# Block 1's first half in another order: eight heads beside the weight slabs, one step a slab, and 512-column matmuls

## The chip, the cores and the metric

One core of one Trainium2 chip runs the whole program in one launch. The metric is the device time of a run in microseconds (us); the kernel before took 3679.07 us, the median of three runs from 3676.93 to 3680.88.

## What is computed

Two pairs of transformer blocks over 256 tokens of width 2048, all in fp32. Activations are kept transposed, with features on the 128 partitions and the 256 tokens on the free axis. One layer of "block 1" is, in the reference (cut):

```python
for i in range(DEPTH):                       # DEPTH = 2
    z = rmsnorm(x, g_mix[i]) @ w_in[i]       # 2048 -> 4928 columns
    (zq, zkv, zkr, sc_b, sc_c, sc_h, cf_a, cf_g, rq, rk, rv, rg) = split_cols(z, IN_SIZES)
    y_a = mla_group(zq, zkv, zkr, ...)       # 4 heads: q, kv from norms of zq, zkv; softmax
    y_b = sc_b * causal_dwconv(sc_c * sc_h, w_sc[i])
    u = causal_dwconv(cf_a * jax.nn.sigmoid(cf_g), w_cf[i], b_cf[i])   # 31 taps
    y_c = jax.nn.silu(layernorm(u, g_cf_ln[i], b_cf_ln[i]))
    y_d = retention_group(rq, rk, rv, rg, ...)   # 4 heads, decays instead of softmax
    x = x + jnp.concatenate([y_a, y_b, y_c, y_d], axis=-1) @ w_o[i]
    uf = causal_dwconv(rmsnorm(x, g_ffn[i]) @ w_up[i], w_ffn_conv[i])
    gate, up = jnp.split(uf, 2, axis=-1)
    x = x + (jax.nn.silu(gate) * up) @ w_down[i]
    x = x + (p[i] @ w_pe[i]) * jax.nn.sigmoid(rmsnorm(x, g_pe[i]) @ w_pg[i])
```

"Block 2" (two more layers) projects a norm of x with w_in_2 to the inputs of four other groups (gla, fox, diff, moba; 16 heads), gates them and multiplies with w_out_2. The first half of block 1 is what stands above the line with w_o.

## The kernel before, in words

**Slabs.** All weights are cut into 636 slabs (`slab_table`, L158 on). A full slab is 16 blocks of 128 inputs by 128 outputs, 1 MB. SP loads slab n into `raw`; ACT copies it, rounded to fp32r, to `whi` (`split_hi`, L970); DVE subtracts, `wlo = raw - whi` (`split_lo`, L1364). There are four buffers (`RAW`), and ACT and DVE split slab n + 3 after PE is done with slab n (`AHEAD`). The activations stand in `H`, per chunk of 128 features, as a high half in columns 0 to 255 and a low half in 256 to 511. PE (`run`, L510) forms, for each of 16 chunks, high weight by both halves and low weight by the high half, into one of four PSUM banks. Where `streams_both` names the slab's matrix, the first two are one 512-column matmul (L531) and both halves lie side by side in the bank, so that DVE has to add them (`folded`, L1381, a TENSOR_REDUCE) before it multiplies by `rms`; elsewhere, that is in the whole first half of block 1, they are two matmuls of 256 columns (L533, L534) that accumulate in one place, and DVE takes the bank with one multiplication (L1390, L1438).

**Order.** Each engine's program is written out by hand, slab by slab: wait for the slab, take its bank, split slab n + 3, then work "beside" it. In block 1's first half the runs are `ret` (12 slabs), `zq` (6), `zkr` (1 of 64 columns), `cfg` (4), `cfa` (4), then 16 small slabs from `w_q_up` and `w_kv_up` (`qn`, `qr`, `kv`), then `sc` (12). The four retention heads run beside zq to cfa, as generators (`ret_heads` on PE, ACT and DVE) that are advanced once or twice a slab; the four MLA heads (`mla_heads`) run beside sc, head after head: sums of squares, spread of the inverse norm, scaling, rotation, scores, softmax, product with the values. The 31-tap convolution of four channel chunks is split: chunks 0 and 1 on DVE (`cf_taps`, L1526, eight taps a sc slab), chunks 2 and 3 on POOL (L469 and L472, 62 steps of a product and a sum). Behind sc stand the layer norm of u and the split of y into `H`, and then `w_o` (`wo`, 16 slabs). Behind wo `norm_h` computes the norm, scales x by it and splits that into `H`, before the first slab of `w_up` can start.

In block 2 the same kind of work is placed by a table (`before_split`, `after_split`, `within_slab`, `after_slab`, `beside_slab`): one step of a head a slab, scores two slabs ahead of the product. Behind its last slab (`gates`) y is gated and split into `H`, and `wout` follows. There the norm is not applied to x: `x_hi` and `x_lo` split x times the gain while `rms` is still being computed, and DVE multiplies the results by `rms`.

## Time and profile before

| | |
|---|---|
| median of three runs | 3679.07 us (3676.93 to 3680.88) |
| the profiled execution | 3682.81 us, its span 3681.0 us |
| PE busy | 3506.0 us, 95% of the span |
| DVE busy | 2588.7 us, 70% |
| ACT busy | 1524.9 us, 41% |
| POOL busy | 971.7 us, 26% |
| mean granted TensorE clock | 0.972 of full speed |
| DMA | 604.06 MB, 164 GB/s |

An engine's busy time is the union of its instructions' spans. Matmuls overlap in the pipeline, so their own durations say less than the distance from one start to the next. The span is 1.8 us shorter than the profiled execution, which itself lies 3.7 us above the median.

### The profile page before, as it was taken

The page shows a single profiled execution, that of the slowest core. Times are in us where ns is not written, and L with a number is a line of the kernel's source. Part 1 is how long each engine was busy: PE and PEld are TensorE (multiplying, and loading weights), DVE is VectorE, ACT ScalarE, POOL GpSimd, SP SyncE. Part 2 cuts the span into 40 slices and gives each one's busy share as a digit, 9 for nine tenths or more (in the row PEclk, how much of TensorE's full clock was granted, in tenths as well). Part 3 has the DMA queues.
Part 4 walks back from the last instruction along what each step waited for, and adds up shares of the span by engine and source line. Part 5 has one row for each costly group of instructions (what it writes and reads, how often), then busy time and mean ns, then how long its engine had stood idle before and what let it go on. Part 6 is the DMA issues. An engine that isn't in the chain of part 4 may idle for free. (4 is left out here: it accounts for less than half of the span.)

```text
span 3681.0 us, 56972 instructions
## 1 busy us (share of the span) xinstructions
PE 3506.0 (95%) x21706; PEld 3093.1 (84%) x21706; DVE 2588.7 (70%) x3400; ACT 1524.9 (41%) x1581; POOL 971.7 (26%) x793
## 2 busy tenths in 40 slices
PE   8988989999999999888899999999999999999998
PEld 7977878888888889877788888888888888878887
DVE  7587577767676765676677676767766866677765
ACT  4432444333433544333444343335444443444442
POOL 3082422212021430553322030313422003140004
PEclk9998999999999999989999999999999999999999
DMA  5332445555555544323455555555543444443443
GB/s 219 138 122 88 152 156 183 174 203 179 198 180 188 190 163 164 133 77 129 150 193 188 188 193 184 193 176 190 177 166 127 150 171 171 166 149 132 155 167 141
DMA packets 93808, 604.06 MB, mean 164 GB/s; under 512 B 10416, under 2 KB 13649, under 8 KB 33105
## 3 DMA queue, kind: packets, MB, share of 16 engines
q1 hardware_dynamic: 92736, 598.78, 46.6%
q10 hardware_dynamic: 912, 3.12, 0.2%
q8 instruction: 105, 1.72, 0.2%
q14 instruction: 55, 0.44, 0.0%
HBM read 599.76 MB, written 2.10 MB: 164 GB/s over the span
## 5 line engine op out<-in xcount | busy, mean ns | idle before, releaser
L531 PE MATMUL bank<-H,whi 128*128 128x512 f32 x6304 | 2247.5, 401 | 44.6 <-DVE H L1444 19.0
L535 PE MATMUL bank<-H,wlo 128*128 128x256 f32 x7552 | 2140.3, 283 | 0.0
L970 ACT ACTIVATE whi<-raw 128x2048 fp32r<-128x2048 f32 (+4 forms) x636 | 1098.5, 1728 | 1180.0 <-DMA raw<-in_slabs_down 274.2
L1364 DVE TENSOR_TENSOR wlo<-raw,whi 128x2048 fp32r<-128x2048 f32 (+4 forms) x636 | 1339.8, 2107 | 250.0 <-ACT whi L970 246.7
L531 PEld LDWEIGHTS bank<-H,whi 128*128 128x128 f32 x6304 | 1192.3, 189 | 343.8 <-issue 37.2
L535 PEld LDWEIGHTS bank<-H,wlo 128*128 128x128 f32 x7552 | 1451.2, 192 | 0.3
L531 PE MATMUL bank<-G,whi 128*128 128x512 f32 x1408 | 488.4, 390 | 0.0
L449 POOL TENSOR_TENSOR sqtmp<-tmp 128x256 f32<-128x256 f32 x88 | 216.6, 2462 | 909.6 <-DVE tmp L1891 909.6
L533 PE MATMUL bank<-H,whi 128*128 128x256 f32 (+1 forms) x1248 | 377.4, 302 | 36.1 <-DVE H L1433 20.9
L535 PE MATMUL bank<-G,wlo 128*128 128x256 f32 x1408 | 397.1, 282 | 0.0
L534 PE MATMUL bank<-H,whi 128*128 128x256 f32 (+1 forms) x1248 | 365.2, 293 | 0.0
L531 PEld LDWEIGHTS bank<-G,whi 128*128 128x128 f32 x1408 | 264.3, 188 | 55.2
L533 PEld LDWEIGHTS bank<-H,whi 128*128 128x128 f32 (+1 forms) x1248 | 250.6, 201 | 44.4 <-DVE wlo L1364 21.3
L1381 DVE TENSOR_REDUCE tmp<-bank 128x256 f32<-128x512 f32 x208 | 143.7, 691 | 183.7 <-PE bank L535 183.4
L535 PEld LDWEIGHTS bank<-G,wlo 128*128 128x128 f32 x1408 | 266.5, 189 | 0.0
L534 PEld LDWEIGHTS bank<-H,whi 128*128 128x128 f32 (+1 forms) x1248 | 250.7, 201 | 0.4
L427 POOL TENSOR_TENSOR sqacc<-sqacc,sqtmp 128x256 f32<-128x256 f32 x135 | 221.9, 1644 | 10.6
L422 POOL TENSOR_TENSOR sqtmp<-x 128x256 f32<-128x256 f32 x135 | 148.0, 1096 | 283.7 <-DVE x L1452 213.4
L1451 DVE TENSOR_TENSOR x<-x,bank 128x256 f32 (+1 forms) x192 | 80.8, 421 | 181.8 <-PE bank L535 180.7
L469 POOL TENSOR_TENSOR sqtmp<-z,cols 128x256 f32<-128x256 f32 (+30 forms) x124 | 97.6, 787 | 338.9 <-DVE z L1833 329.3
L1381 DVE TENSOR_REDUCE z<-bank 128x256 f32<-128x512 f32 x120 | 82.8, 690 | 142.6 <-PE bank L535 141.7
L1305 ACT ACTIVATE G<-sqtmp 128x256 f32 (+1 forms) x88 | 36.8, 418 | 345.6 <-POOL sqtmp L449 345.6
(304 smaller groups left out, 2425.8 us busy)
## 6 DMA issues: line engine op xcount, KB each, us to landing
raw<-in_slabs_up SPq DMA_DIRECT2D x176, 1024.0 KB, 4.8
raw<-in_slabs_down SPq DMA_DIRECT2D x128, 704.0 KB, 4.0
raw<-in_slabs_wo SPq DMA_DIRECT2D x32, 1024.0 KB, 4.8
raw<-in_slabs_pg SPq DMA_DIRECT2D x32, 1024.0 KB, 4.8
raw<-in_slabs_gates SPq DMA_DIRECT2D x32, 1024.0 KB, 4.8
raw<-in_slabs_wout SPq DMA_DIRECT2D x32, 1024.0 KB, 4.8
raw<-in_slabs_ret SPq DMA_DIRECT2D x24, 1024.0 KB, 4.9
raw<-in_slabs_sc SPq DMA_DIRECT2D x24, 1024.0 KB, 4.9
```

Of the source, the lines that this page charges most:

```text
L422: pool.tensor_tensor((sqtmp if c else sqacc)[:], x[:, c, :], x[:, c, :], ALU.mult).then_inc(S("pool_sq"), 1)
L427: ins = pool.tensor_tensor(sqacc[:], sqacc[:], sqtmp[:], ALU.add)
L449: pool.tensor_tensor(act_f[:], tmp[:, 3, :], tmp[:, 2, :], ALU.mult).then_inc(S("act_f32"), 1)
L469: pool.tensor_tensor(sqtmp[:, s:T], u[:, 0:T - s], w, ALU.mult).then_inc(S("cf_product"), 1)
L531: pe.matmul(b[0:r.m, :], whi[:, n % RAW, w], r.src[:, k, :], start=k == 0, stop=False)
L533: pe.matmul(b[0:r.m, 0:T], whi[:, n % RAW, w], r.src[:, k, 0:T], start=k == 0, stop=False)
L534: pe.matmul(b[0:r.m, 0:T], whi[:, n % RAW, w], r.src[:, k, T:2 * T], start=False, stop=False)
L535: last = pe.matmul(b[0:r.m, 0:T], wlo[:, n % RAW, w], r.src[:, k, 0:T], start=False, stop=k == r.kt - 1)
L970: act.activation(whi[:, n % RAW, 0:w], raw[:, n % RAW, 0:w], ACT.Copy).then_inc(S("hi_ready"), 1)
L1364: dve.tensor_tensor(wlo[:, n % RAW, 0:w], raw[:, n % RAW, 0:w], whi[:, n % RAW, 0:w].bitcast(F32), ALU.subtract).then_inc(S("lo_ready"), 1)
L1381: return dve.tensor_reduce(dst, b[0:m, :].rearrange("p (h t) -> p t h", h=2), AX, ALU.add)
L1451: link_in_loop(dve.tensor_tensor(xc, xc, b[:, 0:T], ALU.add), i, j)
```

## The change

1. **Matmuls.** `streams_both` now names all full slabs of the first half: one 512-column and one 256-column matmul a chunk, and `folded` plus a multiplication on DVE for each of 78 slabs. `zkr` becomes a full slab (its 64 columns twice).
2. **Small slabs.** The 16 slabs of qn, qr and kv are three units (`pair_unit`): 8, 4 and 2 output blocks, taken from the banks in pairs by ACT (four) and DVE (three).
3. **Order.** The runs are zq, zkr, cfg, cfa, kv, qn, qr, ret (8), sc (12), rg (4), numbered s = 0 to 41, and the generators give way to a table by s (`behind_first` and `within_first` on PE, `beside_first` on ACT, `before_first` and `after_first` on DVE). MLA heads stand at s = 19 to 24, retention heads at 27 to 33. Keys of all four heads are normed at once, and the inverse norm of the queries goes into the softmax's scale. DVE's taps stand at s = 12 to 30, eight at each of the three units. POOL's taps start behind the third cfa slab as before.
4. **y and w_o.** The layer norm's sums and y's split move in among the last slabs: chunks 0 to 11 of `H` are written while PE is in the last slab (`h_free`), 12 to 15 behind it.
5. **w_o to w_up.** `norm_h` is gone: x is split as in block 2 (`x_hi`, `x_lo`), the norm's sum goes behind the first slab of w_up, and every one of the 176 slabs of w_up gets one more DVE multiplication by `rms`.
6. **Block 2.** Ten of y's 16 chunks are split during the last slab of gates, the other six behind it, and wout takes its chunks in the order in which they come.

```diff
-        add(("ret", l), "w_in", l, DC, P, 12, straight(A_RQ))
         add(("zq", l), "w_in", l, DC, P, 6, straight(A_ZQ))
-        add(("zkr", l), "w_in", l, DC, 64, 1, straight(A_ZKR))
+        add(("zkr", l), "w_in", l, DC, P, 1, [[(A_ZKR, 64), (A_ZKR, 64)]])
         add(("cfg", l), "w_in", l, DC, P, 4, straight(A_CFG))
         add(("cfa", l), "w_in", l, DC, P, 4, straight(A_CFA))
-        add(("qn", l), "w_q_up", l, 4, P, 4, straight(0, 192))
-        add(("qr", l), "w_q_up", l, 4, 64, 4, straight(P, 192))
-        add(("kv", l), "w_kv_up", l, 2, P, 8, straight(0))
+        add(("kv", l), "w_kv_up", l, 2, 8 * P, 1, [[(256 * h + o, P) for o in (0, P) for h in range(HEADS)]])
+        add(("qn", l), "w_q_up", l, 4, 4 * P, 1, [[(192 * h, P) for h in range(HEADS)]])
+        add(("qr", l), "w_q_up", l, 4, 2 * P, 1, [[(192 * h + P, 64) for h in range(HEADS)]])
+        add(("ret", l), "w_in", l, DC, P, 8, straight(A_RQ))
         add(("sc", l), "w_in", l, DC, P, 12, straight(A_SCB))
+        add(("rg", l), "w_in", l, DC, P, 4, straight(A_RG))
...
-    return key[0] in ("wo", "up", "down", "pg", "wout", "gla", "misc", "fox", "diff", "moba", "gates")
+    return key[0] in ("zq", "zkr", "cfg", "cfa", "ret", "sc", "rg", "wo", "up", "down", "pg", "wout", "gla", "misc", "fox", "diff", "moba", "gates")
...
+        def behind_first(l, s):
...
+            if s == 16:
+                key_sums(l)
+                pe.wait_ge(S("unit_taken"), 4 * l + 3)
+                turn_values(12, pS)
+                pe.wait_ge(S("evac"), kv + 1)
+                turn_values(14, pT)
+            if s == 17:
+                spread([((pX, pX, pO, pO)[h][:, (h % 2) * T + t * P:(h % 2) * T + (t + 1) * P], 4 * t + h)
+                        for h in range(HEADS) for t in range(2)])
+            if s == 18:
+                pe.wait_ge(S("values"), 4 * l + 2)
+                pe.wait_ge(S("evac"), kv + 3)
+                turn_halves(vtok[:, P:T], [z[:, 4, :], z[:, 5, :]], pS)
+                query_sums(l)
+            if 20 <= s < 24:
+                turn_probs((s - 20) % 2)
+            if 19 <= s < 23:
...
+                pe.wait_ge(S("query_turned"), l + 1)
+                scores([(z[:, h, :], z[:, 8 + h, :]), (z[half, 4 + h // 2, :], z[half, 6 + h // 2, :])],
+                       (S("keys_scaled"), l + 1))
...
+            if s == 36:
+                pe.wait_ge(S("o_normed"), 2 * l + 2)
+                channel_sums(l)
...
+        def channel_sums(l):
+
+            pe.wait_ge(S("cf_taps"), 31 * len(DVE_CF) * (l + 1))
+            pe.wait_ge(S("cf_pool"), 31 * len(POOL_CF) * (l + 1))
...
+            n = by["kv", l].first
+            for key, base, at, chunk in (("kv", 15, n + 3, 14), ("qn", 16, n + 1, 2), ("qr", 17, n + 2, 4)):
+                for _ in run((key, l), None, base):
+                    dve.tensor_copy(z[:, chunk:chunk + 2, :].rearrange("p a t -> p (a t)"),
+                                    bank[at % 4][:]).then_inc(S("evac"), 1)
+                    advance(taps, 8)
...
+            if s == 40:
+                ret_gated(l, 2)
+                y_lo(0, 0, 12)
+            if s == 41:
+                ret_gated(l, 3)
+                y_lo(0, 12, 16)
...
-            norm_h("g_ffn", l)
+            x_lo("g_ffn", l)
...
-                        link_in_loop(folded(f, b), i, j, 3, 0)
-                        link_in_loop(dve.tensor_scalar(o, f, tap[2], None, ALU.mult), i, j, 3, 1)
+                        link_in_loop(folded(f, b), i, j, 4, 0)
+                        link_in_loop(dve.tensor_tensor(f, f, rms[:], ALU.mult), i, j, 4, 1)
+                        link_in_loop(dve.tensor_scalar(o, f, tap[2], None, ALU.mult), i, j, 4, 2)
```

**Place 1: DVE, the small projections.** Of before, from the last cfa slab on; a COPY takes a bank of qn or qr (L1392), and `wlo` rows are splits of later slabs.

```order
L1438 TENSOR_TENSOR z<-bank,rms 128x256 [waits cf_gate,slab_done]
L1833 TENSOR_TENSOR z<-z 128x256 [waits dve_order]
L1364 TENSOR_TENSOR wlo<-raw,whi 128x512 [waits hi_ready]
L1392 COPY z<-bank 128x256 [waits slab_done]
L1364 TENSOR_TENSOR wlo<-raw,whi 128x512 [waits hi_ready]
L1392 COPY z<-bank 128x256 [waits slab_done]
L1364 TENSOR_TENSOR wlo<-raw,whi 128x256 [waits hi_ready]
```

Now, at the unit qn (s = 16): its pair's copy (L1911), eight taps (L1532; the ones not shown read likewise), the split of the second ret slab (L1394), and only then the inverse norm of the keys (L1437).

```order
L1911 COPY z<-bank 128x512 [waits slab_done]
L1532 SCALAR_TENSOR_TENSOR z<-z,cols 128x236
L1532 SCALAR_TENSOR_TENSOR z<-z,cols 128x235 [waits cf_taps]
...
L1532 SCALAR_TENSOR_TENSOR z<-z,cols 128x229 [waits cf_taps]
L1394 TENSOR_TENSOR wlo<-raw,whi 128x2048 [waits hi_ready,cf_taps]
L1437 RECIPROCAL inv_rms<-inv_rms 128x8 [waits root]
L1911 COPY z<-bank 128x512 [waits slab_done]
```

The taps moved from the sc slabs to the cfa slabs, the units and the ret slabs, ahead of each split.

**Place 2: PE, between the unit qr and the first ret slab, now.** L617 is the last matmul of qr, L635 the spread of the keys' inverse norms, L548 and L552 the first chunk of ret.

```order
L617 MATMUL bank<-cq,wlo 128x256
L635 MATMUL pX<-cst,inv_rms 128x128 [waits inverted]
L635 MATMUL pX<-cst,inv_rms 128x128 x3
L635 MATMUL pO<-cst,inv_rms 128x128 x4
L548 MATMUL bank<-H,whi 128x512 [waits evac,lo_ready]
L552 MATMUL bank<-H,wlo 128x256
```

PE can't begin the ret slab before DVE's reciprocal (L1437) of place 1.

**Place 3: DVE, from the last slab of w_o to w_up.** Before: split, inverse, and the scaled chunks and their low halves in turn.

```order
L1452 TENSOR_TENSOR x<-x,bank 128x256 [waits dve_loop_order]
L1364 TENSOR_TENSOR wlo<-raw,whi 128x2048 [waits hi_ready]
L1402 RECIPROCAL rms<-rms 128x256 [waits rms]
L1420 SCALAR_TENSOR_TENSOR tmp<-x,cols,rms 128x256 [waits dve_order]
L1420 SCALAR_TENSOR_TENSOR tmp<-x,cols,rms 128x256
L1416 TENSOR_TENSOR H<-tmp,H 128x256 [waits h_hi,h_f32]
```

Now:

```order
L1463 TENSOR_TENSOR x<-x,bank 128x256 [waits dve_loop_order]
L1394 TENSOR_TENSOR wlo<-raw,whi 128x2048 [waits hi_ready]
L1444 SCALAR_TENSOR_TENSOR H<-x,cols,H 128x256 [waits h_hi] x16
L1433 RECIPROCAL rms<-rms 128x256 [waits evac,rms,gate_silu,slab_done]
L1411 TENSOR_REDUCE tmp<-bank 128x256 [waits dve_order]
L1956 TENSOR_TENSOR tmp<-tmp,rms 128x256 [waits dve_loop_order]
```

The inverse moved behind the 16 chunks and behind PE's first w_up slab; L1956 is the multiplication that every w_up slab gets.

## Rows read from the trace of the kernel before

**Rows 1.** The page: busy time of each engine, its share of the span, instructions.
```profile
PE 3506.0 (95%) x21706; PEld 3093.1 (84%) x21706; DVE 2588.7 (70%) x3400; ACT 1524.9 (41%) x1581; POOL 971.7 (26%) x793
```

**Rows 2.** Windows: us, busy us of PE, PEld, DVE, ACT, POOL, granted clock, DMA share, GB/s.
```profile
14.07:372.59 358.52, 321.60 (x2306) 303.65 (x2307) 256.65 (x399) 137.96 (x167) 122.12 (x147) 0.93 0.37 132
1335.34:1686.77 351.43, 318.69 (x2306) 302.55 (x2307) 230.04 (x348) 130.52 (x160) 101.06 (x125) 0.91 0.36 123
1489.00:1616.00 127.00, 105.35 (x717) 97.95 (x716) 96.69 (x149) 39.92 (x59) 99.40 (x123) 0.87 0.30 104
1536.00:1687.00 151.00, 126.08 (x773) 113.76 (x772) 119.58 (x200) 50.37 (x78) 74.19 (x90) 0.83 0.25 89
1806.00:1921.00 115.00, 115.00 (x665) 101.44 (x665) 89.10 (x105) 56.35 (x49) 32.99 (x20) 1.00 0.55 192
2644.00:2957.00 313.00, 306.63 (x2126) 259.35 (x2125) 225.80 (x330) 134.17 (x166) 48.79 (x40) 0.98 0.42 149
```

**Rows 3.** Timeline of PE in a ret slab: start us, us, engine, line, operation, tiles.
```profile
1371.83 0.28 PE L533 MATMUL bank<-H,whi 128*128 128x256 f32 x1
...
1372.19 0.28 PE L533 MATMUL bank<-H,whi 128*128 128x256 f32 x1
```

**Rows 4.** Timeline of PE in a w_up slab.
```profile
640.02 0.40 PE L531 MATMUL bank<-H,whi 128*128 128x512 f32 x1
640.26 0.28 PE L535 MATMUL bank<-H,wlo 128*128 128x256 f32 x1
640.37 0.40 PE L531 MATMUL bank<-H,whi 128*128 128x512 f32 x1
```

**Rows 5.** The chain that ended last: 16 sums of squares, one output column each.
```profile
3449.71 1.68 PE pX L817 x16
```

**Rows 6.** Timeline of PE in sc, layer 1: a wait, and the chunks behind it; idle in brackets.
```profile
1620.17 0.90 PE L626 MATMUL pT<-cst,soft 128*128 128x128 f32 x3 [3.20 <-DVE soft L1480]
...
1625.61 0.41 PE L533 MATMUL bank<-H,whi 128*128 128x256 f32 x1
1625.83 0.41 PE L534 MATMUL bank<-H,whi 128*128 128x256 f32 x1
```

**Rows 7.** Timeline of DVE and POOL, taps of layer 1.
```profile
1569.63 5.41 DVE L1526 SCALAR_TENSOR_TENSOR z<-z,cols 128x239 f32<-128x239 f32 x7
...
1575.42 2.36 DVE L1364 TENSOR_TENSOR wlo<-raw,whi 128x2048 fp32r<-128x2048 f32 x1
...
1575.70 2.53 POOL L469 TENSOR_TENSOR sqtmp<-z,cols 128x249 f32<-128x249 f32 x1
...
1579.12 0.60 POOL L469 TENSOR_TENSOR sqtmp<-z,cols 128x248 f32<-128x248 f32 x1
```

**Rows 8.** Timeline of PE: in w_o; to w_up (two); to block 2; to w_out_2.
```profile
1693.57 0.50 PE L531 MATMUL bank<-H,whi 128*128 128x512 f32 x1 [3.12 <-DVE H L1444]
...
1787.37 1.22 PE L567 MATMUL pX<-sqacc,ones 128*128 128x256 f32 x2 [4.38 <-POOL sqacc L427]
1793.87 0.76 PE L531 MATMUL bank<-H,whi 128*128 128x512 f32 x1 [5.28 <-DVE H L1416]
...
3157.00 0.77 PE L531 MATMUL bank<-H,whi 128*128 128x512 f32 x1 [4.77 <-DVE H L1433]
...
3572.55 0.77 PE L531 MATMUL bank<-H,whi 128*128 128x512 f32 x1 [6.09 <-DVE H L1444]
```

**Rows 9.** Timeline of DVE: 16 chunks of H from x, behind w_out_2.
```profile
3155.91 6.88 DVE L1433 SCALAR_TENSOR_TENSOR H<-x,cols,H 128x256 fp32r<-128x256 f32 x16
```

**Rows 10.** Timeline of DVE in two w_up slabs: each one's fold, idle before the second.
```profile
1955.09 0.69 DVE L1381 TENSOR_REDUCE tmp<-bank 128x256 f32<-128x512 f32 x1 [0.65 <-PE bank L535]
...
1960.79 0.69 DVE L1381 TENSOR_REDUCE tmp<-bank 128x256 f32<-128x512 f32 x1 [1.06 <-PE bank L535]
```

**Rows 11.** Timeline of DVE in w_pg slabs: the multiplication by rms.
```profile
2570.68 0.43 DVE L1905 TENSOR_TENSOR tmp<-tmp,rms 128x256 f32<-128x256 f32 x1
...
2582.41 0.93 DVE L1905 TENSOR_TENSOR tmp<-tmp,rms 128x256 f32<-128x256 f32 x1
```

More of the change, by code:

```diff
@@ L335, in groups @@
         full = (r.count - tail) // 4 if r.loop else 0
+        for k in range(4 * r.head):
+            yield k // 4, k % 4
         if full >= 2:
-            with eng.Fori(0, full) as i:
+            with eng.Fori(r.head, full) as i:
                 for j in range(4):
@@ L340, in groups @@
         else:
-            full = 0
+            full = r.head
         for k in range(4 * full, r.count):
@@ L508, in nth, with run @@
             return cnt[name]
-        def run(key, operand=None, beside=None, base=None, free=None):
+        def run(key, operand=None, beside=None, base=None, free=None, order=None):
             r = by[key]
@@ L598, in spread, with pair_unit @@
-        def spread(n):
+        def pair_unit(key, banks, free):
+            r = by[key]
+            n = r.first
+            outs = r.m // P
+            pe.wait_ge(S("lo_ready"), n + 1)
+            for p in range(outs // 2):
+                pe.wait_ge(*free[p])
+                b = bank[banks[p]]
+                for o in range(2):
+                    dst = b[:, o * T:(o + 1) * T]
+                    for k in range(r.kt):
+                        w = slice(r.m * k + P * (2 * p + o), r.m * k + P * (2 * p + o + 1))
+                        pe.matmul(dst, whi[:, n % RAW, w], r.src[:, k, 0:T], start=k == 0, stop=False,
+                                  skip_group_check=True)
+                        pe.matmul(dst, whi[:, n % RAW, w], r.src[:, k, T:2 * T], start=False, stop=False,
+                                  skip_group_check=True)
+                        last = pe.matmul(dst, wlo[:, n % RAW, w], r.src[:, k, 0:T], start=False, stop=k == r.kt - 1,
+                                         skip_group_check=True)
+                last.then_inc(S("slab_done" if 2 * p + 2 == outs else "unit_out"), 1)
@@ new lines, in lora_sums @@
+        def lora_sums(l):
+            pe.wait_ge(S("lora_sq"), l + 1)
+            for first, count, src in ((0, 4, w4[:, 0:4, :]), (2, 2, z[:, 12:14, :])):
+                for t in range(2):
+                    for c in range(count):
+                        last = pe.matmul(pX[:, first + t:first + t + 1], src[:, c, t * P:(t + 1) * P], ones[:, 0:1],
+                                         start=c == 0, stop=c == count - 1, skip_group_check=True)
+            last.then_inc(S("lora_sums"), 1)
@@ L1817, in _ @@
         for l in range(L):
[L1819 to L1829 removed]
+            for key, base in FIRST[:2]:
+                if key == "zq":
+                    to_z((key, l), 0, base=base)
+                else:
+                    for i, j, b in run((key, l), None, base):
+                        link(folded(small[:], b))
+                        dve.tensor_tensor(small[:], small[:], rms[:], ALU.mult).then_inc(S("evac"), 1)
@@ L1830, in _ @@
+            to_z(("cfg", l), 8, base=7)
+            taps = cf_taps(l)
+            for i, j, b in run(("cfa", l), None, 11):
                 c = 4 * i + j
                 dve.wait_ge(S("cf_gate"), 4 * l + c + 1)
-                link(scaled(z[:, 28 + c, :], b))
+                link(folded(z[:, 28 + c, :], b))
+                link(dve.tensor_tensor(z[:, 28 + c, :], z[:, 28 + c, :], rms[:], ALU.mult))
                 dve.tensor_tensor(z[:, 28 + c, :], z[:, 28 + c, :], z[:, 8 + c, :], ALU.mult).then_inc(S("evac"), 1)
-            finish(beside)
@@ L1842, in _ @@
+            to_z(("ret", l), 16, base=18, taps=taps)
+            for i, j, b in run(("sc", l), None, 26):
                 k = 4 * i + j
-                advance(taps, 8)
+                if k == 8:
+                    finish(taps)
+                advance(taps, 3)
                 if k < 8:
-                    scaled(y[:, 4 + k, :] if k < 4 else z[:, 20 + k, :], b).then_inc(S("evac"), 1)
+                    dst = y[:, 4 + k, :] if k < 4 else z[:, 4 + k, :]
+                    link(folded(dst, b))
+                    dve.tensor_tensor(dst, dst, rms[:], ALU.mult).then_inc(S("evac"), 1)
```

843 lines of the change are left out of this document (412 added, 431 removed).

## The prediction

> **What bounds the kernel now.** I read the page first: PE is busy 95% of the span, DVE 70%, POOL 26% [rows 1]. So the time is PE's, and can fall in three ways: fewer or shorter matmuls, less idle time, a higher granted clock. Next the windows. The first half takes 358.5 us in layer 0 and 351.4 in layer 1; in layer 1 PE is idle for 351.43 - 318.69 = 32.7 us at a granted clock of 0.91, and in its last 151 us the clock is 0.83. The mixed part of block 2 takes 313 us for 45 slabs, idle 6.4, clock 0.98 [rows 2]. There the design that the change copies already runs.
>
> Then PE's timeline inside a slab, from start to start. A chunk of three 256-column matmuls takes 0.36 us [rows 3], a chunk of a 512 and a 256 takes 0.35 (0.353 over a slab) [rows 4]: 5.76 against 5.65 us a slab. Waits cost more than their length: behind an idle 3.20 us, matmuls stand 0.22 apart instead of 0.12, still so 5 us after its end [rows 6]. 0.12 is the full 2.4 GHz level and 0.22 about the 1.2 GHz one. I count some 3 us on top of each long wait.
>
> **Matmuls (78 slabs).** 16 x (0.360 - 0.353) = 0.11 us a slab, 9 us in all. The Trainium skill ("TensorE: Matmul & The Clock Gate", § Back-to-back issue gap) gives an isolated matmul N/2.4 + 2.5 ns; an estimate by it is 2.5 ns a chunk, 3 us in all. The sum uses the rows.
>
> **The first half, layer 1, built up anew.**
> - 39 slabs (6 + 1 + 4 + 4 + 8 + 12 + 4) x 5.65 = 220.4 us.
> - The three units: 8 x 2 + 4 x 4 + 2 x 4 = 40 chunks of three matmuls at 0.12 [rows 3] = 14.4 us.
> - Work beside the slabs, with its small waits: in block 2 this is (313 - 45 x 5.65)/45 = 1.30 us a slab [rows 2]. Its price is mostly matmuls of about 0.1 us (16 in 1.68) [rows 5]. The same here: 39 x 1.3 = 51 us. As a check, before had 2306 matmuls [rows 2], of which 38 x 48 + 48 + 120 = 1992 were the slabs'; 314 x 0.105 = 33 us of pure side work, to which waits and clock come.
> - Two places where DVE is the bound, which block 2 has not. At the cfa slabs and units DVE has, from slab s = 13 to the split behind qn, about 1.6 for the bank and the gate, 4 taps and a split; at s = 14 as much work, a little less; then at kv and qn a copy, eight taps and a split each. Taps cost 0.77 each (5.41 for seven), a split 2.36 [rows 7]; 1.6 + 3.1 + 2.4, 6.0, 0.7 + 6.2 + 2.4 and 9.5 make 31.9 us. PE needs 2 x 5.65 + 2 x 5.8 = 23 there. So PE waits some 9 us at the spread of place 2. From there to the turned queries, on which scores at s = 19 wait, DVE has about 21 us against PE's 14: up to 7 more, or the banks and splits absorb it. Part is in the 1.30 already, since PE is ahead by up to three slabs before it stops; I take 3 us on top of 51, and keep 0 and 20 for the range.
>
> 220.4 + 14.4 + 51 + 3 = 289 us, against 351.4: **62 us less**. In layer 0 DVE also prepares tables (its window holds 27 us more DVE and 7 us more time than layer 1's [rows 2]), now beside folded slabs, in which DVE has one instruction more (0.69 [rows 10]); I add 7 + 5: 301 against 358.5, **57 less**. The 9 us of the merged matmuls are inside both.
>
> POOL's taps are costed at nothing. PE needs them at s = 36. POOL did 62 steps in about 127 us (busy 99.4 of the window) [rows 2]; it starts behind s = 13 and PE comes to s = 36 some 165 us later (20 slabs at 5.65 + 1.3, and 26 for the units). What could undo that is a rival below.
>
> **w_o.** Its first slab used to be fed chunk by chunk from y; now 12 of 16 chunks are there when PE arrives. In layer 1 PE stood 3.12 us in it for y [rows 8], with slow matmuls behind. I take 3.5 us a layer: **7 us**.
>
> **w_o to w_up.** PE stood 4.38 us, summed 1.22, stood 5.28; behind w_out_2, where the new scheme runs, it stands 4.77 [rows 8]: 6.1 less. Then `norm_h` fed w_up with two DVE instructions a chunk, and now it is one of 0.43 (6.88 for 16) [rows 9] against PE's 0.35; between 0 and 16 x 0.43 = 6.9 less, I take 4. The sum of squares comes back behind the first slab (1.2) and makes DVE's first bank late, which the four banks hide. 8.7 a layer, **17 us**.
>
> **gates to w_out_2.** The idle 6.09 [rows 8] goes, as ten chunks are ready, and half a microsecond of slow feeding: 6.5 a layer, **13 us**. What is late next is y of the last head; PE then waits inside the slab instead of ahead of it, which I bound at 6 us a layer, gain lost.
>
> **w_up's added multiplication.** 176 times 0.43 to 0.93 us [rows 11] on DVE. DVE is busy 89.1 of 115 us there [rows 2], which is 4.4 a slab of 5.65, and idle 0.65 and 1.06 ahead of two folds [rows 10]. With 0.43 and a gap it takes about 0.55 and DVE stays under 5.65, hidden by its idle time; with 0.93 + 0.15 a slab becomes about 5.8 us, 176 x 0.2 = 35 us longer. The row nearest in form is 0.43, alone in a run of DVE work; 0.93 comes when the instruction meets POOL's. I take 3 us and keep 0 and 35.
>
> **Sum.** 62 + 57 + 7 + 17 + 13 - 3 = 153 us: 3681 - 153 = 3528 of span. The profiled execution is 1.8 above its span and the median 3.7 below the profiled execution, so **3526 us** by the median, 4.2% faster.
>
> **Rivals.**
> 1. *No stall at the units, little waiting* (12%). If banks and splits run ahead enough, the side work is near its bare 33 us rather than 51: 18 us a layer, and the clock with it: about 3480. Against it stand the 31.9 against 23 us at the units.
> 2. *The 512-column matmul is really cheap* (2%). By the rows' durations a chunk is 0.28 + 0.28 - 0.40 = 0.16 shorter, 1248 x 0.16 = 200 us: about 3330. But durations overlap; from the 512's start to the next it is 0.24, twice 0.12 [rows 3, 4]. The Trainium skill ("TensorE: Matmul & The Clock Gate", § Back-to-back issue gap) states about 131 ns a matmul of 512 columns in a stream; by that it would be an estimated 0.11 x 1248 = 137 us. This trace's 0.24 does not agree.
> 3. *POOL is late at s = 36* (7%). A POOL step beside DVE's split takes 2.53 us, else 0.60 to 0.7 [rows 7]. If every one of 62 steps' two instructions met DVE and took 3.3 us a step, it is 205 us against 165: 40 us a layer, about 3604. The Trainium skill ("SBUF — State Buffer", § Who interferes with whom) says that a DVE instruction with two SBUF inputs and a GpSimd one that reads SBUF lock one another out, and splits, taps and the scaling by rms are all of that kind; the 2.53 agrees. Against: the sc stage had as many splits and taps.
> 4. *w_up is bound by DVE* (10%): 0.93 each, 3526 + 32 = 3558.
> 5. *Slower* (2.5%): w_up, where 176 slabs pass. If the added instruction stretches DVE's cycle, by its own time and by the lockout with POOL's 2.5 us products, beyond 5.65 + 0.9 us, the 153 us are used up: at 6.8 us a slab 176 x 1.15 = 202, about 3728. It decides from a new cost of about 2.1 us a slab (0.9 + the 1.2 idle); the rows show at most 0.93.
> 6. *The order stands but stalls stay* (13%): table work in one step a slab makes PE wait at each head as before (32.7 us a layer idle), only the joints gain: about 3600 at worst, 3560 likelier.
>
> **Numbers.** My forecast and its surroundings (3490 to 3550) have 53.5%. The range 3470 to 3575 takes in rival 1, rival 4, the better half of 6 and the bounds 0/20 at the units, 0/6 at w_out_2 and 0/35 in w_up; it leaves out 2, 3, 5 and the rest of 6. A measurement here can tell about 0.2%, 7 us, from no change. Faster 0.96, within 0.2% 0.015, slower 0.025: only rival 5, or 3 and 4 with more that I don't see, reach 3672.
>
> **What would show it.** First half, first matmul of zq to first of w_o: about 300 and 289 us, granted clock 0.96 or more, PE idle 10 to 20 us; a wait of PE at the spread ahead of ret of about 9 us, released by DVE's reciprocal; no wait on POOL at s = 36. w_o to w_up one wait near 5 us; no wait ahead of w_out_2's first matmul over 2 us. w_up slabs at 5.65 us from start to start, with DVE's idle time down from about 1.2 to 0.7 a slab. I am wrong if w_up's slabs exceed 5.75, if the clock of the first half stays at 0.91, or if PE's idle time there is over 30 us.

## The result, and the profile of the changed kernel

The changed kernel took 3563.15 us, the median of four runs (3560.04 to 3568.2), against 3679.98 for the kernel before in the same set: a ratio of 0.9682, with a 95% interval of 0.9664 to 0.9699. It is 3.2% faster. The forecast was 3526 us, 4.2% faster, with a range of 3470 to 3575. The direction and the range held; of the 153 us of the sum 123 came (3681.0 - 3558.2 of span, the profiled execution at 3560.04).

The page of the changed kernel, its line of busy times and that of the granted clock:

```profile
span 3558.2 us, 54218 instructions
...
PE 3435.1 (97%) x20382; PEld 2983.5 (84%) x20382; DVE 2688.8 (76%) x3486; ACT 1477.1 (42%) x1494; POOL 999.3 (28%) x794
...
PEclk8999999999999999999999999999999999999999
```

PE has 71 us less busy time and 52 us less of idle time than in [rows 1]; DVE has 100 us more work. Then the windows, in the order of [rows 2]: first halves of layer 0 and layer 1 from the first matmul of zq to the first of w_o, the stretch of layer 0 behind its second slab, layer 1's units (kv, qn, qr), its ret slabs.

```profile
14.59:341.18 326.59, 296.20 (x1644) 253.34 (x1645) 261.48 (x367) 124.32 (x133) 129.58 (x147) 0.94 0.40 143
1292.60:1590.28 297.68, 285.20 (x1645) 249.34 (x1645) 235.10 (x317) 116.79 (x126) 113.09 (x125) 0.95 0.40 143
37.00:86.00 49.00, 37.51 (x189) 32.36 (x189) 38.47 (x66) 16.02 (x13) 0.00 (x0) 0.84 0.36 129
1384.00:1416.00 32.00, 23.28 (x167) 22.85 (x166) 31.08 (x36) 14.86 (x15) 29.41 (x34) 0.79 0.37 132
1416.00:1484.00 68.00, 65.86 (x357) 55.24 (x356) 54.42 (x79) 21.51 (x33) 62.61 (x69) 0.95 0.31 109
```

The first half fell from 358.5 to 326.6 us in layer 0 and from 351.4 to 297.7 in layer 1. The fourth row is where the time went that layer 1 still lacks: 32 us for 14.4 us of matmuls, DVE busy 31.1 of them, the clock at 0.79. The third row is layer 0's own loss: PE idle 11.5 of 49 us. PE's timeline names the waits, first those of layer 0 (a sum of squares, then a slab, then the sums for q and kv), then the two of layer 1 around the first ret slab:

```profile
42.14 0.59 PE L586 MATMUL pX<-sqacc,ones 128*128 128x256 f32 x2
48.48 0.80 PE L548 MATMUL bank<-H,whi 128*128 128x512 f32 x1 [5.74 <-DVE wlo L1394]
...
79.66 3.55 PE L627 MATMUL pX<-ones,w 128*128 128x1 f32 x16 [5.32 <-ACT z L1090]
...
1412.08 2.08 PE L635 MATMUL pX<-cst,inv_rms 128*128 128x128 f32 x8 [8.72 <-DVE inv_rms L1437]
...
1434.14 2.30 PE L706 MATMUL pS<-z 128*128 128x128 f32 x8 [2.14 <-DVE z L1585]
```

The wait at the spread is the one of place 2: forecast as some 9 us, found as 8.72. DVE's timeline ahead of it has no gap: the eight taps of qn, the split, and only then the reciprocal.

```profile
1402.98 6.23 DVE L1532 SCALAR_TENSOR_TENSOR z<-z,cols 128x236 f32<-128x236 f32 x8
1409.25 2.67 DVE L1394 TENSOR_TENSOR wlo<-raw,whi 128x2048 fp32r<-128x2048 f32 x1
1411.84 0.19 DVE L1437 RECIPROCAL inv_rms<-inv_rms 128x8 f32<-128x8 f32 x1
```

The joints went as forecast. PE's first matmul of w_up waits 4.76 us in both layers, as one wait, in place of the 4.38 and 5.28 of [rows 8]; in w_o's first slab 1.86 us are left of 3.12; w_out_2's first matmul waits for nothing, and inside its first slab 0.93 and 0.72 us are waited.

```profile
439.06 0.52 PE L548 MATMUL bank<-H,whi 128*128 128x512 f32 x1 [4.76 <-DVE H L1444]
...
1596.54 0.50 PE L548 MATMUL bank<-H,whi 128*128 128x512 f32 x1 [1.86 <-DVE H L1455]
...
1686.17 0.77 PE L548 MATMUL bank<-H,whi 128*128 128x512 f32 x1 [4.76 <-DVE H L1444]
```

From the starts of the slabs in both traces I make the balance that answers to the sum. A slab's start is read at its first matmul with the low half of the weights, for the first halves at the first matmul of all; the choice moves a line by up to 0.7 us. Each line is the time of a stretch before less the time after, in us:

| stretch | forecast | found |
|---|---|---|
| first half, layer 1 | 62 | 53.7 |
| first half, layer 0 | 57 | 31.9 |
| w_o, w_o to w_up, first slab of w_up | 7 + 17 | 26.4 |
| gates to w_out_2 | 13 | 14.1 |
| the other slabs of w_up, and w_down | -3 | -11.4 |
| w_pg, w_out_2 and block 2's mixed part | 0 | 8.1 |
| sum | 153 | 122.8 |

So one term is 25 us too high (layer 0), one 8 (layer 1), one 8 too low in cost (w_up, w_down). The 8.1 us of the sixth line nobody forecast. 3.3 of them are in w_pg, whose matmuls the change leaves alone; its slabs happen to stand at the shorter of two distances in this profile (below, with w_down). What made the rest is not shown. Without this line the time would be some 3571 us, still in the range, but by 4 us only. The experiments take the other terms in this order.

### The profile page after: what moved, and what is told of

Read it like the earlier page. It is cut to its first block, busy times and chain, and to the rows that moved or that the text cites. A ratio compares the mean times of both kernels' runs of the same rounds, so it can differ in the third digit from the quotient of the medians.

```text
span 3558.2 us, 54218 instructions
## 1 busy us (share of the span) xinstructions
PE 3435.1 (97%) x20382; PEld 2983.5 (84%) x20382; DVE 2688.8 (76%) x3486; ACT 1477.1 (42%) x1494; POOL 999.3 (28%) x794
## 3 DMA queue, kind: packets, MB, share of 16 engines
q10 hardware_dynamic: 912, 3.12, 0.2%
## 4 chain that ended last, share of the span: by engine, by line
PE 47%; DVE 4%; POOL 2%; ACT 1%; DMA 1%; issue 1%; ACTq 0%; POOLq 0%; DVEq 0%; SPq 0%
PE bank L548 29%; PE bank L552 15%; DVE wlo L1394 1%; POOL w L505 1%; POOL w L504 1%; PE pS L706 0%; ACT whi L1027 0%; DVE H L1455 0%; DVE z L1411 0%; PE pO L744 0%; DVE tmp L1719 0%; DMA raw<-in_slabs_gla 0%; DMA raw<-in_slabs_wout 0%; PE pT L714 0%; PE pS L725 0%
## 5 line engine op out<-in xcount | busy, mean ns | idle before, releaser
L548 PE MATMUL bank<-H,whi 128*128 128x512 f32 x7552 | 2698.3, 401 | 58.7 <-DVE H L1444 41.5
L552 PE MATMUL bank<-H,wlo 128*128 128x256 f32 x7552 | 2129.1, 282 | 0.0
L548 PEld LDWEIGHTS bank<-H,whi 128*128 128x128 f32 x7552 | 1429.1, 189 | 410.1 <-DVE wlo L1394 36.3
L1027 ACT ACTIVATE whi<-raw 128x2048 fp32r<-128x2048 f32 (+1 forms) x610 | 1095.6, 1797 | 1162.3 <-DMA raw<-in_slabs_down 267.2
L1394 DVE TENSOR_TENSOR wlo<-raw,whi 128x2048 fp32r<-128x2048 f32 (+1 forms) x610 | 1340.4, 2198 | 186.3 <-ACT whi L1027 183.0
L552 PEld LDWEIGHTS bank<-H,wlo 128*128 128x128 f32 x7552 | 1439.9, 191 | 0.5
L548 PE MATMUL bank<-G,whi 128*128 128x512 f32 x1408 | 494.6, 393 | 0.0
L552 PE MATMUL bank<-G,wlo 128*128 128x256 f32 x1408 | 398.2, 283 | 0.0
L548 PEld LDWEIGHTS bank<-G,whi 128*128 128x128 f32 x1408 | 264.4, 188 | 61.0
L1411 DVE TENSOR_REDUCE z<-bank 128x256 f32<-128x512 f32 x180 | 124.3, 690 | 201.3 <-PE bank L552 199.8
L552 PEld LDWEIGHTS bank<-G,wlo 128*128 128x128 f32 x1408 | 264.7, 188 | 0.0
L443 POOL TENSOR_TENSOR sqacc<-sqacc,sqtmp 128x256 f32<-128x256 f32 x135 | 218.6, 1619 | 10.6
L438 POOL TENSOR_TENSOR sqacc<-x 128x256 f32<-128x256 f32 x9 | 16.9, 1874 | 615.6 <-DVE x L1463 571.2
L485 POOL TENSOR_TENSOR sqtmp<-z,cols 128x256 f32<-128x256 f32 (+30 forms) x124 | 116.9, 943 | 189.3 <-DVE z L1905 179.6
L488 POOL TENSOR_TENSOR z<-z,sqtmp 128x255 f32<-128x255 f32 (+14 forms) x120 | 103.2, 860 | 9.4
L1958 DVE SCALAR_TENSOR_TENSOR tmp<-tmp,cols 128x255 f32<-128x255 f32 x176 | 85.2, 484 | 20.4 <-DVE tmp L1957 5.9
L1960 DVE SCALAR_TENSOR_TENSOR tmp<-tmp,cols 128x254 f32<-128x254 f32 x176 | 85.1, 483 | 20.1 <-DVE tmp L1958 2.2
```

The costliest lines, as they stand in the source:

```text
L438: pool.tensor_tensor((sqtmp if c else sqacc)[:], x[:, c, :], x[:, c, :], ALU.mult).then_inc(S("pool_sq"), 1)
L443: ins = pool.tensor_tensor(sqacc[:], sqacc[:], sqtmp[:], ALU.add)
L485: pool.tensor_tensor(sqtmp[:, s:T], u[:, 0:T - s], w, ALU.mult).then_inc(S("cf_product"), 1)
L488: pool.tensor_tensor(o[:, s:T], before, sqtmp[:, s:T], ALU.add).then_inc(S("cf_pool"), 1)
L548: pe.matmul(b[0:r.m, :], whi[:, n % RAW, w], r.src[:, k, :], start=at == 0, stop=False)
L552: last = pe.matmul(b[0:r.m, 0:T], wlo[:, n % RAW, w], r.src[:, k, 0:T], start=False, stop=at == r.kt - 1)
```

## Experiments: the wait at the units

Two theories stand for the 8.72 us at the spread. **A**, the order: the reciprocal stands behind taps that could wait. **B**, the amount: DVE has more work from the cfa slabs to the first ret slabs than PE, and the reciprocal is only where this shows. The first run moves the reciprocal alone.

```diff
                                     bank[at % 4][:]).then_inc(S("evac"), 1)
+                    if key == "qn":
+                        invert(8)
                     advance(taps, 8)
...
-            if s == 16:
-                invert(8)
```

> The changed kernel with one move: at the unit qn DVE takes the keys' reciprocal (L1437) ahead of the eight taps and the split, instead of behind them. Theory A, the place of the reciprocal in DVE's order makes PE's 8.7 us wait at the spread: that wait falls under 2 us and the time by 12 to 17 us (two layers). Theory B, DVE's amount of work from cfa to ret is the bound, and the reciprocal only marks where it shows: the wait is gone at the spread but PE waits as long one or two slabs later for a split or a bank, and the time falls by under 5 us.

It took 3569.43 us (3568.74 to 3571.77), ratio to the kernel before 0.97 (0.9684 to 0.9716), 6 us above the changed kernel's median. The wait at the spread is gone, and PE stands somewhere else. Its timeline in that run, and DVE's around the rotated queries:

```profile
1415.24 1.10 PE L667 MATMUL pS<-z,vtok 128*128 128x256 f32 x4 [1.90 <-DVE z L1909]
1436.69 3.82 PE L706 MATMUL pS<-z 128*128 128x128 f32 x8 [8.94 <-DVE z L1585]
```

```profile
1434.48 1.09 DVE L1584 SCALAR_TENSOR_TENSOR z<-z,cols,trig 128x512 f32<-128x512 f32 x1
1435.60 1.04 DVE L1585 TENSOR_TENSOR z<-z,tmp 128x512 f32<-128x512 f32 x1
```

The 8.7 us came back as 8.94, one slab later, ahead of the first scores. DVE's chain from the cfa slabs to this row has hardly a gap, so whatever stands last in it is late. A falls. B's "under 5 us faster" missed by a little, too: the scores behind the later wait run at the lower clock (3.82 us for eight matmuls, 2.30 in the changed kernel), and from qn to the end of ret the two layers together are 2.7 us longer. The rest of the 6 us lies in w_o, w_pg and other stretches that the edit does not touch, and is not explained.

The second run takes work away from the stretch instead: 16 taps a layer go to sc.

```diff
-                    advance(taps, 8)
+                    advance(taps, 8 if key == "kv" else 0)
...
-                advance(taps, 3)
+                advance(taps, 5)
```

> The changed kernel with 16 of DVE's taps a layer (those at qn and qr) moved to the first eight sc slabs, two more in each. Both theories: the wait at the spread goes (12.5 us of DVE work less ahead of it). Theory B (DVE's amount): 16 to 22 us faster in all. Theory A: about as much as with the reciprocal moved, 12 to 17. Against it, if sc had no room on DVE: sc slabs get longer by up to 1.5 us each and eat 10 us or more a layer; DVE is busy 66 of 82 us there, so I expect none.

3550.78 us (3547.33 to 3553.2), ratio 0.9649 (0.9632 to 0.9665), 12 us under the changed kernel. PE's wait at the spread in this run:

```profile
1396.66 2.04 PE L635 MATMUL pX<-cst,inv_rms 128*128 128x128 f32 x8 [1.95 <-DVE inv_rms L1437]
```

By the slabs' starts qr and ret are 11 us shorter in layer 1 (16.3 + 68.2 against 9.6 + 64.4) and 15 in layer 0, and sc is 5 us longer in each: its third and fourth slab take 10.6 and 8.5 us instead of 6.7 and 7.3. I had expected no loss there, from DVE's mean of 66 busy us in 82; slab by slab it has nothing to spare in the third, where the retention heads' decays stand and PE now waits 3.52 us for them. B holds, and its price was an average where a slab was needed.

## Experiments: layer 0's start

Layer 0's zq slabs took 53.6 us and layer 1's 35.2; zkr 16.6 against 8.2. In the kernel before, layer 0 stood only 8 us behind layer 1 in its first run. I named the tables that DVE prepares there. DVE also stands idle for 11.2 us ahead of the first reciprocal of `rms`, and then has everything at once:

```diff
         split_lo(r0, 0, 2, 0)
+        advance(setting, 6)
         inverse()
...
-                advance(setting, 2)
+                advance(setting, 1)
```

> The changed kernel with six of the nine steps of DVE's table set-up in the 11.2 us in which DVE stood idle ahead of the first reciprocal of rms, one step a slab behind it. If the set-up beside the zq slabs is what makes layer 0's first half 29 us longer than layer 1's, it falls by 12 to 18 us. If it is the start (x's loading, the sum of squares) that PE pays for anyway, by under 4.

3556.0 us (3554.27 to 3560.41), ratio 0.9663 (0.9647 to 0.9679): 7 us, not 12. The starts say which part: zkr of layer 0 fell from 16.6 to 8.3 us, and zq, at 54.7, is no shorter. So what the tables cost lay mostly at the end, where 5.32 us of waiting stood ahead of the sums for q and kv. The wait in the third slab had another cause, and the two orders show it. PE's sum of squares for layer 0's norm comes at 42.14 in the changed kernel (above); in the kernel before it came here:

```profile
36.20 0.59 PE L567 MATMUL pX<-sqacc,ones 128*128 128x256 f32 x2
```

Before, it stood behind the second slab. In the table of the change it stands behind s = 2, the third slab (`if s == (2 if l == 0 else 0)`), and DVE's and ACT's next splits wait for its result. I had not seen that one line.

```diff
-            if s == (2 if l == 0 else 0):
+            if s == (1 if l == 0 else 0):
```

> The changed kernel with PE's sum of squares of layer 0 behind the second slab, as in the kernel before, instead of behind the third. POOL has ended the squares by 36.5 us, when PE is at the end of the second slab. If this place is what stops PE for 5.7 us in the third slab and makes layer 0's zq run 53.6 us long (35.2 in layer 1), the time falls by 7 to 12 us. If the start and the tables on DVE set it, by under 3.

3555.63 us (3554.13 to 3560.51), ratio 0.9663 (0.964 to 0.9686), 7.5 us less. PE's timeline:

```profile
36.19 0.62 PE L586 MATMUL pX<-sqacc,ones 128*128 128x256 f32 x2
...
49.56 0.50 PE L548 MATMUL bank<-H,whi 128*128 128x512 f32 x1 [1.08 <-DVE wlo L1394]
```

The 5.74 us are 1.08 now, and zq is 48.1 us. Layer 0's first half is 29 us longer than layer 1's: 18.4 in zq, 8.4 in zkr and 2 elsewhere. The start took 8.4 before already, 8.2 of it in the first two slabs, ahead of any table work (8.7 there now); the place of the sum took 5.5, the tables at zkr 8.3. The 5 us that remain in zq are not separated; DVE takes some 6.6 us a slab there with the tables, which is more than PE's 5.65.

## Experiments: what the 512-column matmuls are worth

```diff
-    return key[0] in ("zq", "zkr", "cfg", "cfa", "ret", "sc", "rg", "wo", "up", "down", "pg", "wout", "gla", "misc", "fox", "diff", "moba", "gates")
+    return key[0] in ("wo", "up", "down", "pg", "wout", "gla", "misc", "fox", "diff", "moba", "gates")
...
-                    link(folded(dst, b))
-                    dve.tensor_tensor(dst, dst, rms[:], ALU.mult).then_inc(S("evac"), 1)
+                    dve.tensor_tensor(dst, b[:, 0:T], rms[:], ALU.mult).then_inc(S("evac"), 1)
```

> The changed kernel with three 256-column matmuls a chunk in the 78 slabs of the first half, as before, and DVE's single multiplication instead of fold and multiplication; the new order and all else stay. By my sum PE pays 0.11 us a slab, 9 us, and DVE gets 0.69 us a slab back, which gives up to 54 us where DVE is the bound and nothing elsewhere: between 9 slower and 10 faster. If the 512-column matmul is worth its difference in duration, 0.16 us a chunk, 140 to 200 us slower.

It took 3552.07 us (3548.39 to 3558.7), ratio 0.9657 (0.9641 to 0.9673): **11 us faster than with the 512-column matmuls**. So the first of the change's six parts costs time. Where PE is the bound, the term was right in kind and small in size: cfa in layer 1 takes 22.2 us merged and 23.0 with three halves, 0.2 us a slab where I had 0.11, rg 24.7 and 25.3. Where DVE is behind, the fold's 0.69 us a slab weigh more: layer 0's zkr falls from 16.6 to 10.8, qr by 2.5 and 1.7, layer 0's ret by 3.3. I had put both parts into the expectation (9 slower to 10 faster) and was 1 us outside it.

The same part alone, in the old order:

```diff
-    return key[0] in ("wo", "up", "down", "pg", "wout", "gla", "misc", "fox", "diff", "moba", "gates")
+    return key[0] in ("ret", "zq", "zkr", "cfg", "cfa", "sc", "wo", "up", "down", "pg", "wout", "gla", "misc", "fox", "diff", "moba", "gates")
...
-            return dve.tensor_tensor(dst, b[0:m, 0:T], rms[0:m, :], ALU.mult)
+            link(folded(dst, b, m))
+            return dve.tensor_tensor(dst, dst, rms[0:m, :], ALU.mult)
```

> The kernel before with one part of the change: the 512-column matmul over both halves in all full slabs of the first half, with DVE's fold, in the old order. PE gains 0.11 us on each of 78 slabs, 9 us. DVE has 0.69 us more on each; where it is the bound (sc, 24 slabs, and layer 0's ret, with the tables) that is up to 25 us lost. After the run of the new order with three 256-column matmuls (11 us faster than the changed kernel) I expect 5 us faster to 15 slower than before.

3695.47 us over ten runs (3682.08 to 3704.52), ratio 1.0042 (1.0028 to 1.0057): 0.4% slower, 1 us outside the expectation. It is a small difference, but the whole interval lies above 1. A window of this run over the sc slabs of layer 1 and the work behind them, four us longer than the one of [rows 2]:

```profile
1535.00:1690.00 155.00, 119.41 (x572) 97.09 (x572) 128.35 (x203) 47.59 (x66) 77.36 (x93) 0.84 0.26 92
```

DVE is busy 128 us of 155 here, 120 of 151 before, PE 119 against 126. The two sc runs are 17 us longer together, and layer 0's ret 4, while the runs in which PE is the bound gain 0.6 to 1.8 each. In both orders, then, the merging is a loss, and the new order gains 117 + 11 us without it.

## Experiments: w_up's multiplication, and the distances in w_down

```diff
-                        link_in_loop(dve.tensor_tensor(f, f, rms[:], ALU.mult), i, j, 4, 1)
```

> The changed kernel without the added multiplication by rms in w_up's 176 slabs (the gate and the values there are left unnormed). By my sum it costs 3 us: 0 to 5 us faster. In the profile of the changed kernel w_down's slabs stand 3.86 us apart (before 3.81) and four of eight w_up runs 5.65 instead of 5.55, 11 us in all: if the multiplication causes that, w_down is at 3.81 again and the time 8 to 12 us less; if it is where the loops and slabs lie, the distances stay.

3562.31 us (3561.01 to 3567.72), 0.8 us under the changed kernel: no difference. The medians alone could hide the 3 us I took, since the runs of one kernel spread over 7 or 8; the slabs can't: in both traces all w_up runs behind the first of a layer stand at the same distances to 0.01 us. The price of the 176 multiplications is nothing that can be seen. The window over w_up slabs in the changed kernel, then in this run:

```profile
750.00:865.00 115.00, 115.00 (x653) 99.74 (x652) 97.66 (x121) 45.28 (x41) 31.92 (x19) 1.00 0.51 182
```

```profile
750.00:865.00 115.00, 115.00 (x652) 99.75 (x652) 86.72 (x104) 47.01 (x40) 29.80 (x19) 1.00 0.52 183
```

11 us of DVE's work in 115, and not one of PE's. In DVE's timeline of the changed kernel the instruction is seen at both its lengths of [rows 11]. Behind the long one the next fold has no wait for PE but still comes 5.56 us after the last, at PE's pace, and the fold after it waits again, so DVE is not the bound:

```profile
759.20 0.43 DVE L1956 TENSOR_TENSOR tmp<-tmp,rms 128x256 f32<-128x256 f32 x1
...
764.29 0.69 DVE L1411 TENSOR_REDUCE tmp<-bank 128x256 f32<-128x512 f32 x1 [0.70 <-PE bank L552]
765.02 0.96 DVE L1956 TENSOR_TENSOR tmp<-tmp,rms 128x256 f32<-128x256 f32 x1
...
769.85 0.69 DVE L1411 TENSOR_REDUCE tmp<-bank 128x256 f32<-128x512 f32 x1
...
775.62 0.69 DVE L1411 TENSOR_REDUCE tmp<-bank 128x256 f32<-128x512 f32 x1 [0.28 <-PE bank L552]
```

The 11.4 us of the table's fifth line have to be something else. They lie in the distance of matmuls with no wait at all. The first matmuls of w_down's first run (16 slabs) and of the w_up run behind it, before and then after:

```profile
734.00 0.39 PE L531 MATMUL bank<-G,whi 128*128 128x512 f32 x1
...
795.02 0.39 PE L531 MATMUL bank<-H,whi 128*128 128x512 f32 x1
```

```profile
685.20 0.39 PE L548 MATMUL bank<-G,whi 128*128 128x512 f32 x1
...
746.98 0.39 PE L548 MATMUL bank<-H,whi 128*128 128x512 f32 x1
```

61.02 against 61.78 us, 3.81 against 3.86 a slab, at a granted clock of 1.00 in both. The w_up runs that follow a w_down run take 5.55 us a slab before and 5.65 after. This is so in the profile of every kernel of either order, 12 of the new and 2 of the old, so in these stretches it goes with the order. It is not a property of the loop's code alone. Layer 0's first two w_up runs go the other way, from 5.65 to 5.55, while layer 1's are at 5.55 in both kernels. And w_pg, which no edit touches, stands in layer 0 at 5.65 us a slab in seven of the fourteen profiles and at 5.55 in the other seven, in each for the whole run of slabs. One property that I could change is where the loops begin in the round of four buffers and banks:

```diff
+        add(("pad", l), "w_pe", l, 2, P, 1, straight(0))
         add(("wo", l), "w_o", l, DC, P, DC, straight(0))
...
+            pe.wait_ge(S("p_ready"), 4)
+            run(("pad", l))
...
+            for _, _, b in run(("pad", l)):
+                dve.tensor_copy(small[:], b[:, 0:T]).then_inc(S("evac"), 1)
```

> The run with 512-column matmuls where DVE is idle, and one small slab more in each layer ahead of w_o (two chunks of w_pe, whose product nobody uses), so that w_down's loops begin at slab numbers that leave 3 and 0 when divided by four, as in the kernel before, instead of 2 and 2; four buffers and four banks follow the slab's number. All runs so far have w_down at 3.81 us a slab with the first, 3.86 with the second. If the numbering sets it, w_down is at 3.81 and most w_up runs at 5.55, 11 to 16 us less, against about 4 us for the two slabs: 5 to 12 us faster in all. If it is something else in the program, the distances stay and the time is 2 to 6 us longer.

3532.8 us (3530.0 to 3537.53), ratio 0.9594 (0.9578 to 0.961), 7 us above the run that it was built on (below), where the expectation for another cause was 2 to 6; the two small slabs take 4.7 and 4.2 us by the starts. w_down's first run, from its first matmul to w_up's:

```profile
663.05 0.39 PE L549 MATMUL bank<-G,whi 128*128 128x512 f32 x1
...
724.83 0.39 PE L549 MATMUL bank<-H,whi 128*128 128x512 f32 x1
```

61.78 again. The numbering is not the cause. What is stays open. The stretch lost 11.4 us where the forecast had 3, so 8 of the 30 us that the forecast was off lie there.

## Experiment: the split of y ahead of w_out_2

```diff
-            if s == 59:
-                y_lo(1, 0, 10)
...
-                y_lo(1, 10, 16)
+                y_lo(1, 0, 16)
```

> The changed kernel with DVE's ten low halves of y that stand in the last slab of gates moved behind them, to the other six. If PE's 6.1 and 6.7 us of waiting ahead of w_out_2 in the kernel before went by this edit alone, 5 to 13 us slower than the changed kernel. If ten chunks written a slab earlier only serve to keep DVE free, 0 to 3 slower.

3566.71 us (3562.73 to 3573.9), ratio 0.9694 (0.9668 to 0.972): 3.6 us slower by the medians, between the two expectations and within the intervals. The trace shows it more sharply, as PE's wait ahead of w_out_2's first matmul (2.62 us in the other layer):

```profile
2951.35 0.47 PE L548 MATMUL bank<-H,whi 128*128 128x512 f32 x1 [2.74 <-DVE H L1455]
```

2.74 and 2.62 us come back of 6.7 and 6.1. The gates run is 3 us longer in each layer (99.3 against 96.3), not the 7 that it was before. The other 4 us a layer must come from the rest of part 6 (ACT's halves written in the last slab, the gating placed earlier, the order in which w_out_2 takes its chunks), which I did not separate.

## Experiments: the parts that helped, together

Three kernels with the taps moved (34 of the 40 a layer that are left for sc stand in its slabs 5 to 9, 27 of them in 5 to 8, which the expectation gives as 24; none in the third and fourth), six steps of the tables ahead of the first reciprocal, and the sum one slab earlier.

```diff
-                if k == 8:
+                if k == 9:
                     finish(taps)
-                advance(taps, 3)
+                advance(taps, (3, 3, 0, 0, 5, 7, 6, 9, 7, 0, 0, 0)[k])
```

> The changed kernel with everything that helped: no taps at qn and qr (24 of the 40 left for sc stand in its slabs 5 to 8, none in 2 and 3, where the run with later taps waited), tables ahead of the first reciprocal, the sum one slab earlier, and three 256-column matmuls in the first half. If the moves add up: 12 + 5 (the two long sc slabs) + 7 + 7.5 under the changed kernel's 3563, and 5 of the 11 us of the three halves, whose rest was at the tables and is gone: about 3526. If DVE's total work bounds the first half whatever the order, they overlap and it stays above 3540.

> As the run before, but with the changed kernel's 512-column matmuls. If those cost time only where DVE is behind: 3528 to 3535, that is 2 to 9 us above the run before. If the new places of the taps leave DVE enough time everywhere, it is 5 to 9 us below it, by PE's 0.11 us a slab.

> As the two before, with the 512-column matmul in zq, zkr, cfg and rg (15 slabs a layer), where DVE waits for PE, and three of 256 in cfa, ret and sc. It should be the lowest of the three, 2 to 4 us below the run with three halves throughout; if it is not, DVE's waiting in a slab is no sign that it has time there.

| matmuls of the first half | us, median of five | ratio to before |
|---|---|---|
| three halves | 3527.84 (3524.31 to 3530.6) | 0.9575 (0.956 to 0.9589) |
| 512 columns in all | 3527.83 (3527.6 to 3535.7) | 0.9578 (0.9564 to 0.9592) |
| 512 columns in zq, zkr, cfg, rg | 3525.73 (3520.32 to 3530.75) | 0.9569 (0.9553 to 0.9585) |

All three are 35 to 37 us under the changed kernel, 4.3% under the kernel before. Between them nothing can be told, their intervals overlap: once tables and taps no longer make DVE late, the form of the matmul is worth no more than these runs resolve. The first came 2 us above the 3526 of "if the moves add up", so they do not overlap much. The merged kernel came out between its two expected cases. The one with both forms is lowest, but by 2 us. The last kernel's window over layer 1's units and the two cfa slabs ahead of them, and its spread:

```profile
1352.00:1384.00 32.00, 32.00 (x256) 31.82 (x256) 29.53 (x33) 16.05 (x16) 24.82 (x25) 0.95 0.43 158
```

```profile
1381.34 1.05 PE L635 MATMUL pX<-cst,inv_rms 128*128 128x128 f32 x8
```

PE has no idle time where it had 8.7 us. Over the units alone, 1362.5 to 1383, the clock is 0.92 instead of 0.78 and PE never idle, and they still take 21.1 us: 6.7 above the 14.4 of their matmuls, for the side work and the part at the lower clock. The sc run is back at 81.5 us with more taps in it. One part did not come. DVE's reciprocal and PE's next wait in this kernel:

```profile
31.36 0.70 DVE L1839 CAST y<-y 128x256 f32<-128x256 int32 x1
...
44.19 1.75 DVE L1433 RECIPROCAL rms<-rms 128x256 f32<-128x256 f32 x1
```

```profile
37.27 0.59 PE L586 MATMUL pX<-sqacc,ones 128*128 128x256 f32 x2
49.39 0.80 PE L548 MATMUL bank<-H,whi 128*128 128x512 f32 x1 [5.97 <-DVE wlo L1394]
```

With the sum at 37 us the reciprocal could stand at 38, but six steps of the tables fill DVE until 44, and zq is as long as in the changed kernel. Two or three steps ahead of it and the rest behind should give the 5 us of the earlier sum as well; it was not tried. That the total came out near 3526 all the same is luck in part: with the 7.5 us of the sum missing, qn to sc are 30 us shorter in the first of the three kernels, both layers together, where the expectation had 12 + 5 + 5.

## Why the prediction was right, and where it was not

- **What bounds the kernel, and the build-up of layer 1: right.** 39 slabs at 5.65 and the units make 234.8 us; I added 51 for the work beside them and 3 for the stall. Found: 31.8 us from kv to the first ret slab, where 14.4 had been put, and 297.7 - 31.8 - 220.4 = 45.5 for the rest. Block 2's 1.30 us a slab was a good price, 1.17.
- **The step that failed in layer 1** is "Part is in the 1.30 already ...; I take 3 us on top". I had counted 9 and 7 us for the two places at which DVE is the bound, found them in the order, and then gave them away. Found are a wait of 8.72 and one of 2.14, and units of 31.8 us. Without the stall, in the last kernel above, the units take 21.1, so it costs 10.7 there with the slow clock. The counted 16 was the nearer term: it would have given 302 us, against 297.7 found and 289 forecast. DVE's work was summed from rows, and PE cannot run ahead over it, as the run with the moved reciprocal shows.
- **The step that failed in layer 0** is "I add 7 + 5". It should have been 29. The 7 by which the kernel before was longer in layer 0 stood, as 8.4; the tables' 5 were 8.3 by the run with the tables first, and up to 5 more in zq. And 5.5 us were no cost of DVE's at all but a line in PE's table that puts the sum behind the third slab, which none of my terms held. To these 17 us layer 1's 8 come again.
- **Merged matmuls.** That they are worth a tenth or two of a us a slab and not 0.16 a chunk: right, and rival 2 with its 200 us is out; at the 0.2 found in cfa all 78 slabs would give 16. The sign of the part as a whole was wrong, because I costed DVE's fold at nothing but in layer 0. By the two runs its price where DVE is behind exceeds PE's gain, by 11 us in the new order and 16 in the old.
- **The joints: right,** 26.4 for 24 and 14.1 for 13.
- **w_up: right in kind,** the multiplication is hidden and free; rivals 4 and 5 are out. The 11.4 us there are a term that I did not have.
- **POOL at s = 36:** no wait for it is in the trace. Its products still meet DVE (2.50 us instead of 0.57, as in [rows 7]), and it ends in the third sc slab in layer 1, eight slabs ahead of need. Rival 3 is out. What the same lockout does to DVE is under the last heading.
- **Rivals 1 and 6** did not come. The units do stall, against 1. Layer 0's gain alone, 31.9 us of the 57, would fit 6, but its waits stand at the start, the sum and the tables, and not at each head.
- **The signs that I named.** The first half's clock is 0.94 and 0.95, not 0.96 or more. PE's idle time is 12.5 us in layer 1, as said, but 30.4 in layer 0, just over the 30 that I had called a sign of being wrong: it was one, of layer 0's term. The w_up slabs are at 5.55 to 5.65, under 5.75, and DVE's idle time there is 0.85 us a slab, where I had 0.7.
- **Slips in the sums.** The small slabs of the kernel before have 144 matmuls and not 120, so the check should read 2016 and 290 x 0.105 = 30 us, not 1992 and 33. And 4.38 + 1.22 + 5.28 - 4.77 + 4 - 1.2 is 8.9 us and not 8.7. Neither moves the forecast by more than half a us.

## What to carry to other kernels

Where a stretch is bound by the amount of work on the second engine, moving its late instruction forward moves the wait and not the end; sum that engine's work from the rows between two points that the first engine must pass, and do not discount it by an average from another stage. Move work out slab by slab, by the idle time of each slab and not of the stage. And a faster form of the first engine's instruction that gives the second one more to do is to be costed on both, stage by stage.
